# Order of the first loads of a fused transformer block: chunks and weight units in turn, half chunks later, and two operand steps moved

## What is computed

```
mod = silu(c) @ w_ada + b_ada          # 2048 -> 6*2048: shift, scale, gate for mixer and MLP
h   = rms_norm(x) * (1 + sc_a) + sh_a  # the operand of the first product
p   = h @ w_in                         # 2048 -> 4096 columns (padded): latent q/kv, stick-breaking, forgetting q,k,v
...                                    # latent products, three kinds of attention, w_out, gate g_a
h   = rms_norm(x) * (1 + sc_m) + sh_m
x   = x + g_m * (relu(h @ w_ff1)**2 @ w_ff2)
```

## Time and profile before

| | us |
|---|---|
| median of the runs | 1185.87 |
| the profiled execution | 1181.04 |
| its span (first to last instruction) | 1179.2 |

### The profile page before, as it was taken

One profiled execution on the slowest core, in us unless ns is written; L12 is line 12 of the kernel. 1 busy time (PEld: TensorE's weight loads), 2 busy tenths in 40 slices (PEclk: granted clock), 3 DMA queues, 4 the chain that ended last, 5 costly groups with the idle time before them and its releaser, 6 DMA issues.

```text
span 1179.2 us, 21533 instructions
## 1 busy us (share of the span) xinstructions
PE 1113.4 (94%) x9084; PEld 1072.6 (91%) x9084; DVE 744.3 (63%) x898; ACT 519.0 (44%) x627; POOL 295.5 (25%) x143
## 2 busy tenths in 40 slices
PE   7889998797998996999999999999999999999995
PEld 6779888786778996999999999999999999999995
DVE  5588658676876667877877455454555555455454
ACT  3644443365454434544444433333444454344341
POOL 3869886465405792000000000000000000000000
PEclk8999999988999998999999999999999999999998
DMA  9999978699662897588787655555566665655631
GB/s 383 415 415 392 372 316 321 215 339 374 232 217 71 341 409 303 217 305 292 277 303 250 200 196 195 197 194 191 190 196 188 202 195 188 196 194 186 204 126 72
DMA packets 76703, 296.86 MB, mean 252 GB/s; under 512 B 8513, under 2 KB 8641, under 8 KB 72513
## 3 DMA queue, kind: packets, MB, share of 16 engines
q1 hardware_dynamic: 76608, 295.50, 69.8%
HBM read 293.37 MB, written 2.10 MB: 251 GB/s over the span
## 4 chain that ended last, share of the span: by engine, by line
PE 76%; DMA 8%; DVE 7%; issue 4%; ACT 3%; POOL 1%; SPq 0%; DVEq 0%; ACTq 0%
PE ps L1219 44%; PE ps L1225 22%; DMA ada<-in_ada 5%; PE ps L1390 3%; DMA raw<-in_weights 2%; PE ps L1237 2%; DVE ada L808 1%; PE ps L1242 1%; DVE qk L874 1%; DVE o_tok L1122 1%; PE ps L1282 1%; POOL w_lo L711 1%; DVE ada_more L808 1%; ACT tmp L463 1%; ACT w_hi L431 1%
## 5 line engine op out<-in xcount | busy, mean ns | idle before, releaser
L431 ACT ACTIVATE w_hi<-raw 128x1024 fp32r<-128x1024 f32 x362 | 380.9, 1059 | 480.7 <-PE ps L1225 405.1
L787 DVE TENSOR_TENSOR w_lo<-raw,w_hi 128x1024 fp32r<-128x1024 f32 x256 | 315.2, 1240 | 265.0 <-ACT w_hi L431 264.3
L1219 PE MATMUL ps<-hT,w_hi 128*128 128x256 f32 x3072 | 384.7, 278 | 16.9 <-issue 6.4
L1219 PEld LDWEIGHTS ps<-hT,w_hi 128*128 128x128 f32 x3072 | 366.6, 189 | 21.1 <-issue 7.4
L711 POOL TENSOR_TENSOR w_lo<-raw,w_hi 128x1024 fp32r<-128x1024 f32 x106 | 256.8, 2434 | 105.3 <-ACT w_hi L431 104.6
L1219 PE MATMUL ps<-act,w_hi 128*128 128x256 f32 x2048 | 252.9, 276 | 0.0
L1219 PEld LDWEIGHTS ps<-act,w_hi 128*128 128x128 f32 x2048 | 241.6, 188 | 0.0
L1225 PE MATMUL ps<-hT,w_lo 128*128 128x256 f32 x1536 | 206.1, 277 | 1.8 <-POOL w_lo L711 1.8
L1225 PEld LDWEIGHTS ps<-hT,w_lo 128*128 128x128 f32 x1536 | 189.0, 188 | 2.1 <-POOL w_lo L711 2.1
L705 POOL TENSOR_TENSOR ssq<-ssq,sq 128x1024 f32<-128x1024 f32 x6 | 14.4, 2404 | 657.3 <-ACT sq L438 657.3
L1225 PE MATMUL ps<-act,w_lo 128*128 128x256 f32 x1024 | 136.9, 276 | 0.0
(11 more groups left out here) (200 smaller groups left out, 801.5 us busy)
## 6 DMA issues: line engine op xcount, KB each, us to landing
raw<-in_weights SPq DMA_DIRECT2D x362, 512.0 KB, 4.5
ada<-in_ada SPq DMA_DIRECT2D x128, 512.0 KB, 5.3
ada<-in_whole SPq DMA_DIRECT2D x16, 1024.0 KB, 8.8
ada_more<-in_whole SPq DMA_DIRECT2D x16, 1024.0 KB, 11.1
xT<-in_xt SPq DMA_DIRECT2D x4, 512.0 KB, 7.2
y<-tmp SPq DMA_DIRECT2D x2, 512.0 KB, 2.6
consts<-in_consts SPq DMA_DIRECT2D x1, 580.0 KB, 6.3
y<-sq SPq DMA_DIRECT2D x1, 512.0 KB, 2.6
```

The source lines that it names most:

```text
L431: sc.activation(w_hi[:, u % RING, :, :], raw[:, u % LOADS, :, :], ACT.Copy).then_inc(hi_done, 1)
L787: ve.tensor_tensor(w_lo[:, slot, :, :], raw[:, u % LOADS, :, :], w_hi[:, slot, :, :].bitcast(F32), ALU.subtract).then_inc(lo_vec, 1)
L1219: pe.matmul(acc[:, n, :], w, rhs[:, kt0 + k, half, :], start=first and k == 0 and n % 2 == 0 and half == 0, stop=False, skip_group_check=True)
```

## The change

Three edits, all within the first 240 us.

1. `ada_ahead` and `ADA_STOPS`: from the first unit on, chunk and unit are issued in another order: a1 a2 u0 a3 u1 u2 a4 u3 a5 u4 u5 a6 u6 a7 u7 u8 a8 u9 a9 u10 a10 u11 a11 u12 a12 u13 a13 u14 a14 u15 a15 u16 u17 a16 u18 u19 a17 ..; from u18 on each whole chunk is issued two units sooner than before. The half chunks follow later: a31 u48 u49 .. u56 without a chunk between, then a32 a33 u57 a34 u58 a35 u59 a36 u60 a37 a38 u61 a39 u62 a40 u63 a41 u64 a42 a43 u65 a44 u66 a45 u67 a46 u68 a47 a48 u69 a49 u70 a50 u71. VectorE reduces a4 to a7 in blocks 0 to 3 of part 0, a8, a9, a10 in blocks 5, 6, 7, and a11, a12 in blocks 0 and 2 of part 1 (before: a4 to a7 in blocks 1 to 4, a8 and a9 in 6 and 7, a10, a11, a12 in blocks 0, 1 and 3 of part 1). From a13 on the places are as before.
2. `mix_gain(1)` and `mix_operand(1)` move from block 5 of part 0 to block 4.
3. `mix_lo(1)` moves from block 6 of part 0 to block 7, behind that block's first chunk, which is now a10.

```diff
-ADA_STOPS = ((4, 4, 5, 6, 7, 8, 8, 9, 10), (10, 11, 12, 12, 13, 14, 15, 16, 16),
+ADA_STOPS = ((4, 5, 6, 7, 8, 8, 9, 10, 11), (11, 12, 12, 13, 13, 14, 15, 16, 16),
...
+AHEAD_FIRST = (3, 4, 4, 5, 6, 6, 7, 8, 8)
+
+
 def ada_ahead(u):
 
-    if u < 6:
-        return 3 + u
-    return min(8 + (8 * (u - 6) + 12) // 13, 16 + max(0, u - 18) // 2) if u < 51 else 32 + 3 * (u - 51) // 2
+    if u < 9:
+        return AHEAD_FIRST[u]
+    if u < 17:
+        return u
+    return min(A_GA, 16 + (u - 16) // 2) if u < 57 else 34 + 5 * (u - 57) // 4
...
-                    if p == 0 and b == 5:
+                    if p == 0 and b == 4:
                         mix_operand(1)
...
-                        if p == 0 and b == 5:
+                        if p == 0 and b == 4:
                             mix_gain(1)
...
-                        if p == 0 and b == 6:
+                        if p == 0 and b == 7:
                             mix_lo(1)
```

## The result

The changed kernel takes 1188.3 us (median of 20 runs) against 1186.6 us for the kernel before, run beside it. The ratio is 1.0026, with a 95% interval of 1.0014 to 1.0038: slower by 3.1 us, where 3.1 us faster had been forecast. Its profiled execution took 1188.51 us, its span 1186.7. Some executions of nearly every kernel here are disturbed and over 1% longer: the medians hold them, the ratios leave them out, and of the four experiments whose profile was such a one (the first of the tail, the two units without gates, both of the last version) only places up to unit 66 are used.

A forecast was written before the change was run, and what follows sets the result against it. TensorE, 94% busy, was taken to stand for late loads: full DMA engines up to part 2, then one queue held by waiting chunks. +2.6 + 0 + 1.3 - 7.0 = -3.1 us, from 1185.87 to 1182.8 us; range 1179.0 to 1188.4.

The forecast's parts named there:

- Start, +2.6: Parts 0 and 1: unit 16 lands one MiB later, so its matmuls start at 84.9 us instead of 82.29; +2.6 us.
- the bound of 2.2: Lower bound on the +2.6 us loss forecast for unit 16's start; the upper bound was +3.2.
- Counting bytes: Loads up to part 2 land by the bytes issued ahead, about 2.5 us per MiB.
- the rival by which landing does not go by position: Pieces in flight overlap, unit 16 lands where it did, +2.6 falls away: 1180.2 us; chance 0.14.
- Parts 2 and 3, 0: Units from 18 on come 2.5 us later, like TensorE itself; the seven-slot ring hides chunk waits; value 0, bounds 0 and +2.
- Part 4, +1.3: Half chunks issued later delay VectorE, so unit 56 starts at 204.5 against 203.23 us; bounds 0 and +5.7.
- rival 1: Lower TensorE clock follows the new waits; a slow unit 56 costs 1.7 to 1.9 us: 1184.6 us; chance 0.18.
- rival 2: Part 4: late half chunks starve VectorE, unit 56 starts +5.7 and slow (+1.8): total +3.1, 1189.0 us; chance 0.15.
- Units 64 and 65 on time, -7.0: Latent stage: ScalarE no longer waits for these units' weights; first scores at 234.8 instead of 240.51 us; -7.0, bounds -8.5, -3.5.
- Handover, 0: Stage behind the first scores, 240 to 290 us: moves as a whole with VectorE's start; value 0.
- Rival 3: Bytes bind from 240 to 290 us, so half of the 7.0 us goes: 1186.3 us, no change; chance 0.13.

The follow-up runs named there:

- the tail: Kernel before with its order up to unit 50 and the changed kernel's order from there, run twice; ratios 0.9998 and 0.9982.
- the two units without gates: Kernel before with units 55 and 56 ahead of chunk 36, later units two half chunks sooner or more, no waits added on GpSimd; ratio 0.9999.
- the last version: The version with two gates, with half chunks 32 and 33 issued behind unit 51 and reduced in part 3; ratios 0.9861 and 0.9900 to the kernel before.
- unit 16 put back: Changed kernel with unit 16 issued ahead of chunk 15 again, its byte position in the kernel before; ratio 1.0004 to the kernel before.
- The gates: Changed kernel with two GpSimd waits, holding the low parts of units 63 and 64 for VectorE's latent steps; ratio 0.9991 to the kernel before.
- the low part back: Changed kernel without edit 3: pair 1's low part back in block 6, ahead of chunk 10; ratio 1.0005 to the kernel before.
- the version with two gates: Kernel before with units 55, 56 ahead of chunk 36, later units sooner, unit 67 ahead of chunk 51, GpSimd waits for units 63, 64; ratio 0.9899.
- the start alone: Changed kernel's order up to unit 49 with edits 2 and 3, half chunks in the order of before; ratio 1.0016 to the kernel before.

## Why the prediction was wrong, point by point

- **Start, +2.6.** Right in mechanism and size: unit 16 landed at 71.69 (72.0 forecast) and started 2.15 us late, a hair under the bound of 2.2. (The page of before lists 580 KB of constants, not 0.2 MiB; that shifts every position alike and changes no difference.) Counting bytes held here; the rival by which landing does not go by position did not occur. Its statement that edits 2 and 3 don't reach unit 16 holds in the changed kernel, but by less than I thought: with the landing put back, a slow unit 8 behind edit 3's stop still kept unit 16 at 83.7.
- **Parts 2 and 3, 0.** Right: the 2.15 us pass through unchanged.
- **Part 4, +1.3.** The sum "Unit 56 starts at 204.5 against 203.23" was mis-sized: from unit 16 to unit 56 the loss is 5.15 - 2.15 = 3.0 us. I had written that VectorE wants chunk 37 at 186.6 and stands, and then followed only the last chunk before unit 56. The intermediate addition, block 1's, was late as well, and unit 54 waits for it. The tail alone shows it, 1.4 us after its own drift is taken off. The issue times were right (chunk 42's unit 64 went at 197.42, forecast 195.3 + 2.15); the landings were not: "the first lands 3.5 us after its issue" gave chunk 37 for 191.6 and chunk 42 for 203.1 with the shift, and they came at 193.4 and 205.6. The size in the changed kernel's profile is that of one profile: from unit 48 to unit 56, 29.9 us before, the same tail took 31.6 to 31.8 in the five other profiles that have it and 32.9 in after, so 1.3 was short by some 0.5 there, and by 1.7 in after. The lower clock behind that stop, rival 1's mechanism at a place where I had no stop, is on top of it (3.67 us against 2.0 for unit 54's first 16 matmuls). Of rival 2, the starved VectorE, the direction was right and the size (+5.7) was not: chunk 42 was reduced from 205.59, 2.15 of which are the start's.
- **Units 64 and 65 on time, -7.0.** This is the step that failed. "`latent(0)` needs `add_block(4, 6)`, which ends at 227.46, in the new order 228.8" took VectorE's durations of before for granted. Measured from unit 56 to the first scores the change brought +0.6 instead of -7.0. The stop of unit 65 did go; but the same early loads let GpSimd work beside VectorE's latent steps, which grew by 2.0 and 2.65 us on the path to unit 62 and unit 64. The gates gave 3.4 us back by timing alone. The miss of 7.6 us adds up: 4.7 for the two steps of VectorE (4.1 against before, whose unit 64 waited another 0.6 us for its load, counted as gained in the forecast), 1.6 for units 56 and 57 at the lower clock (7.2 us for both, 5.6 before), 1.3 for units 64 and 65 (7.3 us to the scores, 6.0 forecast).
- **The clock, rival 1.** Five profiles without gates have the changed tail. Against before, they lose between unit 48 and the first scores -0.6 us (unit 16 put back), 0.8 and 0.9 (the tail, twice), 2.3 (the low part back) and 3.6 (after). The first has no slow unit among 54, 56 and 64; the two of the tail have one each (56, then 64), the next has 56 and 64, and after has all three. So each costs about 1.3 to 1.5 us, somewhat less than rival 1's 1.7 to 1.9, and even without any the tail gives 0.6 us where 5.7 (7.0 - 1.3) were forecast: the two steps of VectorE (4.7) and the landings (0.5) account for the 5.1 between.
- **Handover, 0.** Nearly right: between the first scores and the read of the attention's output the delay grows from 5.75 to 6.3 us. Rival 3, bytes that bind there, is not what happened: the DMA share of that stage fell to 0.86 (0.94 before), and an earlier start was kept almost whole in the version with two gates.
- **No rival had the collision.** All four dealt with bytes and the clock. I never asked what GpSimd's work costs VectorE, though the trace of before already shows two low parts at 2.18 us where one alone takes 0.69, and the earlier trace rows have that very instruction at 1.34, with a low part of GpSimd running from 70.63 to 73.02. That rival 2's total, +3.1 us, is what was measured is luck: it was made of other terms.

What stays open: why the lower clock strikes unit 56 in some profiles and not in others behind the same stop (2.02, 2.06 and 2.10 us: slow in after, with the gates, and with the low part back; 2.01, 2.03, 2.09 and 2.10 us: not slow in the start alone, in before, with unit 16 put back, and in the second profile of the tail), how often it does so in executions that were not profiled, and so how the 3.1 us of the ratio divide between the clock and the rest.

## What to carry to other kernels

When a load comes sooner, follow the instruction that it releases on every engine, and ask what runs at that moment on the engine that shares a port with it; a wait for data can be what kept two engines apart. Follow a starved engine through all its steps, not only the last one before the stage's end: the first late addition stopped TensorE here. And where two limits end together, measure each before pricing the removal of one.

## What the runs showed of the hardware

- VectorE beside GpSimd's low parts (128x1024, 2.4 us each) waits for them: four scalings 128x256 take 3.7 us instead of 1.67, two low parts 128x512 take 4.83 instead of 1.29, and a `TENSOR_SCALAR` 8x256 takes up to 2.10 instead of 0.34. One `SCALAR_TENSOR_TENSOR` 128x512 (line 827 of before) takes 2.77 in every kernel here, always beside a low part, where two instructions of its size just ahead take 0.69 each; it was never seen alone. The additions of 128x1024, which read PSUM, stay at 1.2 us throughout. GpSimd pays a little too: two of its low parts take 5.47 and 5.19 us there, where two times 2.41 would be 4.8.
- The granted clock behind a stop of TensorE isn't decided by the stop's length alone: behind 2.10 us unit 56's 8 matmuls took 2.10 us in the tail alone and 2.86 with the low part back. The lower level is 1.2 GHz, the higher 2.4.
